# Hybrid decoder step: the output projection's LRU half on operands without the norm's root, and softplus of dt on 128 partitions by way of DRAM

## The reference, cut to what matters

```
xn = rmsnorm(h);  proj = xn @ w_in  ->  z, xbc, dt, gate, xl
xbc = silu(causal_conv(xbc));  dt = softplus(dt + dt_bias)       # 16 heads
a_cs = cumsum(dt * -exp(a_log)) per chunk of 128 tokens (per sample of 4)
y = SSD scan of xbc with dt and a_cs;  y_ssd = rmsnorm(y * silu(z))
xl = causal_conv(xl);  r, i = sigmoid(block gates of xl)
hs = linear recurrence, a = exp(-8 * r * softplus(-lambda))
y_lru = rmsnorm(hs * gelu(gate), norm_lru)                       # width 1024
h = h + concat(y_ssd, y_lru) @ w_out
h = h + PEER experts(rmsnorm(h));  h = h + gated embedding;  final rmsnorm
```

## Time and profile before

| what | value |
|---|---|
| median of 3 runs | 1906.53 us |
| the profiled execution | 1902.72 us |
| its span in the trace | 1901.0 us |
| PE busy | 1796.1 us (94%) |
| DVE busy | 1507.3 us (79%) |
| ACT busy | 837.1 us (44%) |
| the mixer's last matmuls | about 446 to 449 us |

### The profile page before, as it was taken

One profiled execution on the slowest core, in us unless ns is written; L12 is line 12 of the kernel. 1 busy time (PEld: TensorE's weight loads), 2 busy tenths in 40 slices (PEclk: granted clock), 3 DMA queues, 4 the chain that ended last, 5 costly groups with the idle time before them and its releaser, 6 DMA issues.

```text
span 1901.0 us, 29713 instructions
## 1 busy us (share of the span) xinstructions
PE 1796.1 (94%) x11394; PEld 1732.9 (91%) x11394; DVE 1507.3 (79%) x2723; ACT 837.1 (44%) x1202; POOL 522.0 (27%) x415
## 2 busy tenths in 40 slices
...
GB/s 143 91 67 79 116 118 99 51 56 179 112 128 146 145 169 227 234 295 345 361 362 373 352 353 359 367 392 376 380 367 380 376 394 379 375 338 340 205 56 48
DMA packets 163772, 462.68 MB, mean 243 GB/s; under 512 B 16624, under 2 KB 76720, under 8 KB 160944
## 3 DMA queue, kind: packets, MB, share of 16 engines
...
...
## 4 chain that ended last, share of the span: by engine, by line
PE 71%; DVE 13%; DMA 10%; ACT 3%; issue 2%; SPq 0%; POOL 0%; DVEq 0%; ACTq 0%
PE PS L454 12%; PE PS L1477 8%; PE PS L1478 7%; PE PS L1479 7%; DMA Rw<-vn 7%; PE PS L1490 6%; PE PS L1492 6%; PE PS L1491 6%; PE PS L1466 5%; PE PS L1543 4%; PE PS L2049 2%; DVE Hl L1853 1%; ACT Rh L164 1%; DVE Rl L169 1%; DVE ug L1861 1%
## 5 line engine op out<-in xcount | busy, mean ns | idle before, releaser
L169 DVE TENSOR_TENSOR Rl<-Rw,Rh 128x1024 fp32r<-128x1024 f32 x272 | 332.4, 1223 | 162.2 <-ACT Rh L164 154.8
L164 ACT CAST Rh<-Rw 128x1024 fp32r<-128x1024 f32 x272 | 284.1, 1045 | 389.4 <-PE PS L1492 343.8
L1432 POOL DMA_INDIRECT ug<-un,idxU x160 | 241.6, 1510 | 579.7 <-DVE dots L1861 353.9
L1490 PE MATMUL PS<-Hh,Rh 128*128 128x384 f32 x1024 | 352.2, 344 | 39.3 <-DVE Hl L1853 39.0
L1477 PE MATMUL PS<-Xh,Rh 128*128 128x384 f32 x1016 | 351.2, 346 | 3.8 <-DVE Rl L169 2.8
L1491 PE MATMUL PS<-Hl,Rh 128*128 128x384 f32 x1024 | 349.2, 341 | 0.0
L1492 PE MATMUL PS<-Hh,Rl 128*128 128x384 f32 x1024 | 349.0, 341 | 0.0
L1478 PE MATMUL PS<-Xl,Rh 128*128 128x384 f32 x1016 | 342.3, 337 | 0.0
L1479 PE MATMUL PS<-Xh,Rl 128*128 128x384 f32 x1016 | 341.3, 336 | 0.0
L1432 POOL DMA_INDIRECT ug<-vn,idxU x160 | 234.1, 1463 | 280.6 <-DVE yacc L1866 215.8
L1490 PEld LDWEIGHTS PS<-Hh,Rh 128*128 128x128 f32 x1024 | 194.9, 190 | 48.7 <-issue 48.5
...
## 6 DMA issues: line engine op xcount, KB each, us to landing
...
Rw<-vn SPq DMA_DIRECT2D x128, 512.0 KB
...
acts<-Ab SPq DMA_DIRECT2D x128, 192.0 KB
...
```

The lines of the kernel that those rows point to most:

```text
L164: a.copy(self.Rh[:, q, :], self.Rw[:, q, :]).then_inc(self.S("rhi"), 1)
L169: v.tensor_tensor(self.Rl[:, q, :], self.Rw[:, q, :], self.Rh[:, q, :].bitcast(F32), ALU.subtract).then_inc(self.S("rlo"), 1)
L1432: p.indirect_dma_start(out=ug[:, r % 4, :], out_offset=None, in_=un if r < IDC else vn, in_offset=bass.IndirectOffsetOnAxis(ap=idxU[:, r % ...
L1490: pe.matmul(out, Rh[:, q, w], hh, start=(g == 0), stop=False)
```

## The change

Softplus: `dts` is written to DRAM and read back so that 16 rows of 544 become 128 rows of 68 (`dtw[:, 6]`), and the result goes back the same way into `dts`. SP issues the first pair of transfers behind its load of tile 3, the second behind its load of tile 8, and waits within each pair. ACT's and DVE's parts stand one or two passes later (3, 4, 5, 6); product, scan and `wts` stay on 16 partitions and stand in pass 8, the exponentials of `wts` in pass 9.

LRU half: `ylh` and `yll` are made from `gg` times `norm_lru` alone; `lru_add` becomes two DVE operations, the PSUM result times `rstdL` into `tmpL`, and the sum with h. The squares 0 to 3 are taken in pass 21 (`sq4l`), DVE adds six of the eight squares (`lru_sum`) and PE sums three inputs behind tile 27. `BTb` and `CBs` stand ahead of `scores(0)` in pass 35, `CBm` in pass 32.

```diff
@@ -212,7 +212,8 @@
-    dtw = at("dtw", A5, [NH, 6, T])
+    dtw = at("dtw", A5, [P, 7, T // 8])
+    dA = at("dA", A5 + T * 4, [NH, T])
     smask = at("smask", A5 + 6 * T * 4, [NH, T])
@@ -240,6 +241,8 @@
     sq8l = at("sq8l", AT + SL, [P, ND, T])
+    sq4l = at("sq4l", A5, [P, 4, T])
+    tmpL = at("tmpL", sh.free + 2 * SL + T * 4, [P, T])
     ce = at("ce", A6, [P, 2, HG, P])
@@ -287,6 +292,16 @@
             load(n)
+            if n == 3:
+                sp.wait_ge(S("dt_v"), 2)
+                sp.dma_start(dtd, dts[:, :]).then_inc(S("dtm"), 16)
+                sp.wait_ge(S("dtm"), 16)
+                sp.dma_start(dtw[:, 6, :], dtd.rearrange("h (q t) -> (h q) t", q=8)).then_inc(S("dtm"), 16)
+            if n == 8:
+                sp.wait_ge(S("spv"), 19)
+                sp.dma_start(spd.rearrange("h (q t) -> (h q) t", q=8), dtw[:, 5, :]).then_inc(S("dtm"), 16)
+                sp.wait_ge(S("dtm"), 48)
+                sp.dma_start(dts[:, :], spd).then_inc(S("dtm"), 16)
             if n == 4:
@@ -427,7 +442,7 @@
             elif n < OS0:
-                pe.wait_ge(S("ole"), n - OL0 + 1)
+                pe.wait_ge(S("ole"), 2 * (n - OL0) + 1)
             else:
@@ -478,6 +493,15 @@
+        def lru_sums():
+            pe.wait_ge(S("sqz"), ND + 4)
+            pe.wait_ge(S("sq_ready"), 2 * ND)
+            for src, first, last in ((tmpL[:, :], True, False), (sq8l[:, 6, :], False, False),
+                                     (sq8l[:, 7, :], False, True)):
+                for q in range(2):
+                    m = pe.matmul(pair(3)[:, q, :], ones[:, :], src[:, q * HT:(q + 1) * HT], start=first, stop=last)
+            m.then_inc(S("sq_free"), ND)
+
         def sums(r, k, src):
@@ -601,9 +625,8 @@
                 token_scalars()
-            if n == 26:
-                for k in range(ND):
-                    sums(1, k, sq8l[:, k, :])
+            if n == 27:
+                lru_sums()
             if n == 28:
@@ -668,6 +691,8 @@
                 a.wait_ge(S("loo"), 4)
+            if i == ND + 2:
+                a.wait_ge(S("sqz"), ND + 2)
             a.activation(dst[:, 0:NP], ctmp[:, s, 0:NP], func).then_inc(S("act_c"), 1)
@@ -697,6 +722,9 @@
             a.activation(dst, src, ACT.Square).then_inc(S("sq_ready"), 1)
+
+        def lru_hi(k):
+            a.activation(ylh[:, k, :], gg[:, k, :], ACT.Copy, scale=col("norm_lru", k)).then_inc(S("ylh"), 1)
@@ -737,27 +765,25 @@
                 hi(n + 1)
-            if n == 2:
+            if n == 3:
                 a.preload_act_table(ACT.Exp)
-                a.wait_ge(S("dt_v"), 2)
-                a.activation(dtw[:, 0, :], dts[:, :], ACT.Abs).then_inc(S("spa"), 1)
+                a.wait_ge(S("dtm"), 32)
+                a.activation(dtw[:, 0, :], dtw[:, 6, :], ACT.Abs).then_inc(S("spa"), 1)
                 a.activation(lv[:, 0, :], col("lam", 0, ND), ACT.Abs).then_inc(S("spa"), 1)
...
                 a.activation(hv[:, 2:3], hv[:, 1:2], ACT.Exp).then_inc(S("spa"), 1)
-            if n == 4:
+            if n == 5:
                 a.wait_ge(S("spv"), 2)
...
                 a.activation(lv[:, 2, :], lv[:, 1, :], ACT.Ln).then_inc(S("spa"), 1)
-            if n == 7:
+            if n == 9:
                 a.wait_ge(S("spv"), 26)
...
             if GA0 < n <= ZZ0:
-                if n == GA0 + 1:
-                    a.wait_ge(S("spv"), 27)
                 sigmoids(n - GA0 - 1)
@@ -794,11 +820,18 @@
                     root(m)
+                a.wait_ge(S("ylr"), 4)
+                for k in range(4):
+                    lru_hi(k)
+                    square(1, k, sq4l[:, k, :], gg[:, k, :])
             if n == 25:
                 a.wait_ge(S("scan"), ND)
-                for k in range(ND):
+                for k in range(4, ND):
                     a.wait_ge(S("ylr"), k + 1)
                     square(1, k, sq8l[:, k, :], gg[:, k, :])
+            if n == 27:
+                for k in range(4, ND):
+                    lru_hi(k)
             if n in (26, 27):
@@ -809,10 +842,6 @@
                 a.preload_act_table(ACT.Silu)
-            if n in (31, 32):
-                for k in range(4 * (n - 31), 4 * (n - 31) + 4):
-                    a.wait_ge(S("normed"), k + 1)
-                    a.copy(ylh[:, k, :], gg[:, k, :]).then_inc(S("ylh"), 1)
             if n == 30:
@@ -944,15 +973,18 @@
-        def lru_norm(k):
-            v.wait_ge(S("rst"), 2)
-            v.scalar_tensor_tensor(out=gg[:, k, :], in0=gg[:, k, :], scalar=col("norm_lru", k), in1=rstdL[:, :],
-                                   op0=ALU.mult, op1=ALU.mult).then_inc(S("normed"), 1)
-
         def lru_lo(k):
             v.wait_ge(S("ylh"), k + 1)
-            v.tensor_tensor(yll[:, k, :], gg[:, k, :], ylh[:, k, :].bitcast(F32), ALU.subtract
-                            ).then_inc(S("yll"), 1)
+            v.wait_ge(S("sq_ready"), ND + k + 1)
+            v.scalar_tensor_tensor(out=yll[:, k, :], in0=gg[:, k, :], scalar=col("norm_lru", k),
+                                   in1=ylh[:, k, :].bitcast(F32), op0=ALU.mult, op1=ALU.subtract
+                                   ).then_inc(S("yll"), 1)
+
+        def lru_sum(k):
+            v.wait_ge(S("sq_ready"), ND + k + 1)
+            v.wait_ge(S("sqz"), ND + k - 2)
+            v.tensor_tensor(tmpL[:, :], sq4l[:, 0, :] if k == 1 else tmpL[:, :],
+                            sq4l[:, k, :] if k < 4 else sq8l[:, k, :], ALU.add).then_inc(S("sqz"), 1)
@@ -1015,8 +1047,12 @@
             v.wait_ge(S("mm"), n + 1)
-            hs = halves(h[:, d, :])
-            v.tensor_tensor(hs, hs, pair(n % 2), ALU.add).then_inc(S("ole"), 1)
+            v.wait_ge(S("rst"), 2)
+            if d >= 1:
+                v.wait_ge(S("ole"), 2 * d)
+            v.tensor_tensor(halves(tmpL[:, :]), pair(n % 2), halves(rstdL[:, :]), ALU.mult).then_inc(S("ole"), 1)
+            v.wait_ge(S("ole"), 2 * d + 1)
+            v.tensor_tensor(h[:, d, :], h[:, d, :], tmpL[:, :], ALU.add).then_inc(S("ole"), 1)
@@ -1135,15 +1170,18 @@
                 v.wait_ge(w, 18)
-                v.scalar_tensor_tensor(out=dts[:, :], in0=dts[:, :], scalar=0.0, in1=dtw[:, 5, :], op0=ALU.max,
-                                       op1=ALU.add).then_inc(w, 1)
+                v.scalar_tensor_tensor(out=dtw[:, 5, :], in0=dtw[:, 6, :], scalar=0.0, in1=dtw[:, 5, :],
+                                       op0=ALU.max, op1=ALU.add).then_inc(w, 1)
                 v.tensor_tensor(lv[:, 5, :], lv[:, 5, :], lv[:, 6, :], ALU.add).then_inc(w, 1)
                 v.wait_ge(w, 20)
-                v.tensor_scalar(dtw[:, 4, :], dts[:, :], hv[:, 3:4], None, ALU.mult).then_inc(w, 1)
                 v.tensor_scalar(spl[:, 0, :], lv[:, 5, :], -8.0, None, ALU.mult).then_inc(w, 1)
                 v.tensor_scalar(spl[:, 1, :], lv[:, 5, :], 8.0, None, ALU.mult).then_inc(w, 1)
+            if n == 8:
+                v.wait_ge(S("dtm"), 64)
+                v.tensor_scalar(dA[:, :], dts[:, :], hv[:, 3:4], None, ALU.mult).then_inc(w, 1)
                 v.wait_ge(w, 23)
-                v.tensor_tensor_scan(out=acs[:, :], data0=smask[:, :], data1=dtw[:, 4, :], initial=0.0, op0=ALU.mult,
+                v.wait_ge(S("const"), 28)
+                v.tensor_tensor_scan(out=acs[:, :], data0=smask[:, :], data1=dA[:, :], initial=0.0, op0=ALU.mult,
                                      op1=ALU.add).then_inc(w, 1)
@@ -1195,19 +1233,31 @@
                                   xs[r, 9, NP:T].rearrange("p (b t) -> p b t", b=NB)).then_inc(S("bcz"), 1)
-            if n in (30, 31):
-                for k in range(4 * (n - 30), 4 * (n - 30) + 4):
-                    lru_norm(k)
-            if n in (32, 33):
-                for k in range(4 * (n - 32), 4 * (n - 32) + 4):
-                    lru_lo(k)
+            if n in (24, 25):
+                lru_lo(2 * n - 48)
+                lru_lo(2 * n - 47)
+            if n == 25:
+                for k in range(1, 4):
+                    lru_sum(k)
+            if n == 26:
+                lru_sum(4)
+                lru_sum(5)
+            if n in (28, 30):
+                lru_lo(n - 24)
+                lru_lo(n - 23)
             if n == 33:
                 l_min(0)
+            if n == 32:
                 for b in range(2):
...
                                     mask[:, :].unsqueeze(1).broadcast_to([P, 4, P]), ALU.mult).then_inc(S("cbm"), 1)
+            if n == 35:
+                v.wait_ge(S("cbp"), 4)
+                v.tensor_tensor(CBs[:, :], PS[0:64, 6, 0:32], mask2[:, :], ALU.mult).then_inc(S("cbm"), 1)
+                v.tensor_tensor(BTb[:, :, :], PS[0:64, 6, P:2 * P].unsqueeze(1).broadcast_to([64, NB, P]),
+                                segm[:, :].unsqueeze(2).broadcast_to([64, NB, P]), ALU.mult).then_inc(S("cbm"), 1)
             if n == 35:
```

More of the change, by code:

```diff
@@ L1219, in vector @@
                 v.tensor_tensor(Ls[:, :, :], Ls[:, :, :], am, ALU.subtract).then_inc(S("lss"), 1)
-            if n == 35:
-                v.wait_ge(S("cbp"), 4)
```

(3 more changed lines are left out.)

25 lines of the change are left out of this document (13 added, 12 removed).

## The result

The changed kernel takes 1886.42 us (median of 4 runs, 1884.01 to 1890.32) beside 1906.1 us for the kernel before (4 runs, 1904.52 to 1908.59): ratio 0.9900, 95% interval 0.9877 to 0.9923. The forecast was 1890.5, with a range of 1884.5 to 1898.5. The profiled execution took 1887.0 us, its span is 1885.3: 15.7 us less than before's 1901.0, where 16.0 were forecast.

A forecast was written before the change was run, and what follows sets the result against it. PE, carrying 71% of the chain of waits, was taken as the bound, with the change in the mixer. 5.4 + 13.2 - 1.7 - 0.65 - 0.3 = 16.0 us off the median 1906.53 gave 1890.5, range 1884.5 to 1898.5.

The forecast's parts named there:

- Softplus: Tiles 3 to 10: softplus on 128 partitions removes PE's waits ahead of tiles 5 and 7; gain 5.4 us.
- The straight line between the two reciprocals: Softplus on DVE: interpolating 3.54 us for 544 columns and 0.13 for 8 gives 0.51 us for 68.
- Up to chunk 1's transposes: LRU half: fewer sums, less DVE work, earlier `BTb`; chunk 0 17.8 us ahead, chunk 1 13.2 ahead.
- Clock before tile 37: After chunk 1's transposes: PE, idle for 5 us, begins tile 37 at the lower clock; -1.7 us.
- Step (e): Behind 300 us: `lru_add`'s second DVE operation is hidden, except at the `ce` wait (-0.65 us) and ahead of tile 43 (-0.3).
- Tile 43: Ahead of tile 43, where PE waits for `yl`: the chain over `Wlo` is 0.3 us later.
- Behind the mixer: From about 460 us on: this part is shifted as a whole, with no gain of its own.
- B: Rival: tile 4's weight load lands late, PE waits 6.8 us and the clock drops; 1898 us, chance 0.12.
- C: Rival: DVE stays late in tiles 25 to 36, PE waits some 4 us, clock drops once; 1896 us, chance 0.08.
- D: Rival: no clock drop before tile 37 and shorter waits; gain 18 to 21 us, 1886 to 1888.5, chance 0.12.
- E: Rival: the later stages, paced by the experts' DMA, take the gain back, leaving below 4 us; chance 0.05.
- F: Rival: the clock stays down after the 4.4 us wait ahead of the `xs` transposes; slower, 1915 us, chance 0.03.

The follow-up runs named there:

- E5: Kernel before with the softplus steps in the change's new passes, but on 16 partitions and without the trip to DRAM: 1900.27 us, ratio 0.9977.
- E2: Kernel before with the LRU half and the moves of `BTb`, `CBs` and `CBm`, softplus as it was: 1894.61 us, ratio 0.9948.
- E3: Kernel before with only `CBs` and `BTb` moved ahead of `scores(0)` in DVE's pass 35: 1903.07 us, ratio 0.9998.
- E10: Changed kernel with PE summing all eight squares and DVE's additions left out: 1889.08 us, ratio 0.9919.
- E9: Changed kernel with two extra writes of `dts` to DRAM, waited for ahead of tile 4's load: 1889.94 us, ratio 0.9932.
- E4: Changed kernel with `BTb` and `CBs` put back behind `scores(0)`, `l_min(1)` and `Ls`: 1881.74 us, ratio 0.9895.
- E1: Kernel before with only the softplus part of the change (buffers, four transfers, passes): 1893.45 us, ratio 0.9935.
- E0: Changed kernel run again, unedited, on the same chip as its three variants: 1884.22 us, ratio 0.9917.
- E8: Changed kernel with chunk 3's `ce` transfer one tile earlier and chunk 0's state copy ahead of `scores(1)`, run twice: 1877.96 and 1878.12 us.
- E6: Changed kernel with SP issuing chunk 3's `ce` transfer behind the load of tile 40, not 41: 1883.90 us, ratio 0.9912.
- E7: Changed kernel with chunk 0's state copy ahead of `scores(1)` and `l_min(2)` in DVE's pass 36: 1884.43 us, ratio 0.9916.

## Why the prediction was right, and where it was not

- **Softplus, forecast 5.4.** Measured at the first gate 6.5, of which 0.5 was there already when tile 3 started (32.44, 31.96): 6.0. E5 shows that the new place alone doesn't make it. The mis-sized term is the trip to DRAM: I took the one `acsd` of the earlier trace rows, 2.8 us, and the four trips took 1.5 to 1.7. That price belonged to the moment and not to the transfer. In the kernel before, E2 and E3 SP issues `acsd` directly behind the load of a weight tile (0.5 us later), and it takes 2.8 to 3.1 us; in the other eleven traces it is issued about 3 us behind that load and takes 1.6. The Trainium skill (DMA: Bandwidth & Descriptors, Anatomy of one DMA), with about 2.0 us for the fixed part, was nearer than that row; by the measurement the figure is a little high for 34 KB, and the page gives it for transfers that GpSimd issues, where these are SP's. Of the 1.0 us of waiting that the price implied at most 0.2 came, and 0.4 in E10; E9 brought a wait back by adding the missing time. The straight line between the two reciprocals (0.51) held: 0.58.
- **Up to chunk 1's transposes, forecast 13.2.** Measured 19.3 less 6.5: 12.8. Chunk 0 was forecast at 257 with a wait of 4.4 (256.72, 4.36), chunk 1 16.6 later (16.54). What that step says of causes is shown by E10 (4.6 us of sums, whole) and by E3 and E4 (the order of `BTb`: 1.6 or 1.7 at chunk 1, nothing later). The 3.79 us ahead of tile 35 are gone in all kernels with the LRU half, and stand in E1, E3 and E5.
- **Clock before tile 37, forecast -1.7.** Chunk 2's gain is 2.2 below chunk 1's (2.8 in E0). The drop is confirmed by its absence in E4 and E8, where the wait ahead of chunk 1 is 0.74 and 0.76 (the tile behind it at 1.00).
- **Step (e), the chain over `ce`, forecast -0.65: this step failed.** It assumed that the transfer lands as fast as before. DVE's row had 6.32 us of waiting, and the chain ended 0.1 us ahead of PE: I added the one DVE operation of 0.7 and nothing for the transfer. Both halves of the chain were longer. SP issued the transfer 9.8 us behind the start of chunk 2's transposes, 8.6 before: 0.8 is the second DVE operation, and 0.4 lies between SP's load of the weight tile and its issue of the transfer (303.93 to 304.71), where before had

```profile
320.21 0.33 SPq L270 DMA_DIRECT2D Wr<-wm  x1
320.58 1.09 SPq L273 DMA_DIRECT2D ce<-eacd  x2
```

These 0.4 us stand in E1 too, and not in E2 or E9; what makes them is not shown. And from the first issue to DVE's read it was 6.9 us in this trace (304.71 to 311.63), and 5.9 in that of before. In the chain of waits the second of the two transfers stands as

```profile
305.21 6.39 DMA ce<-eacd
```

where before's two took 4.9 and 5.4 us, and E0's second one 5.59; 2 MB for `s0s` are issued right behind it in both kernels, and why it landed later is not shown. The late issue is in both traces of the changed kernel; the landing was 1.0 us slower than before in the first and 0.2 in E0: the wait for PE was 2.28, 1.49, 2.39 and 2.59 us in the changed kernel's two traces, E9 and E10. In all four the lower clock followed (0.67 to 0.83 over 10 us), which (e) did not count. Together 2.2 us at the transposes and up to 2.9 more by tile 43. E6 takes the chain away, and both parts of the loss with it.
- **Tile 43, forecast -0.3.** The wait is 2.44 in place of 2.18, as forecast. The lower clock behind it was not: the wait of 2.44 or 2.45 stands in all ten traces with the LRU half, and the granted clock over the 8 us behind it was 0.79 in six of them (the changed kernel, E7, E8 twice, E9, E10) and 1.00 in E0, E2, E4 and E6. It cost 1.5 us in the changed kernel (tile 43's gain of 12.0 is 10.4 at the last matmul), and nothing in E0. The mixer's sum as measured is 6.5 + 12.8 - 2.2 - 2.2 - 2.9 - 1.5, which makes 10.4 with unrounded terms, where 16.0 was forecast.
- **Behind the mixer, forecast 0.** This stretch was 5.3 us shorter. Over the 14 traces of this study it lies between 1445.2 (E4) and 1458.0 (E2), though its code is the same. PE's longest group of waits there, for `Hl` of the experts, moves along with it on the whole. That row is, for the kernel before, the changed kernel, E4 and E2:

```profile
PE PS L1490 <- DVE Hl L1853: 39.0, 13, 17.5
```
```profile
PE PS L1535 <- DVE Hl L1898: 35.8, 15, 15.3
```
```profile
PE PS L1535 <- DVE Hl L1898: 32.6, 13, 15.1
```
```profile
PE PS L1522 <- DVE Hl L1885: 41.2, 17, 16.0
```

(us in total, times, longest). The kernels whose mixer ends early have the shorter stretch on the whole (E8 1446.0 and 1448.7, E3 1457.4, E5 1455.1), but E9 has 1457.6, E1, with a late mixer, 1450.5, and E4, with a later mixer than E8, 1445.2. E0 came to 1449.8, within 0.5 of the first trace: that is what the rival of its expectation asked for (a property of this kernel), though E9, with the same code there, is 8 us off. The times of all runs bear on it too. Taken as us (the ratio's interval times the median before), the first set gave 14.7 to 23.4 us less, E1 7.8 to 17.1, both above what the mixer gave in the traces (10.4 to 13.4, and 3.9); E0's 11.2 to 20.3 takes in its 13.4. So more than the mixer's gain is there in the mean of the runs, and chance alone is the less likely reading; what in the experts would gain from an earlier start, no run here shows, and it stays open. It also sets how far the forecast of 1890.5 was right for its reasons: by the mixer alone, with its 10.4 to 13.4 us, the changed kernel would be at 1893 to 1896 from a median of 1906.5.

Of the rivals, B (late load) did not come, though E9 shows how near it was; C did not; D failed at its condition, since the clock did drop, though the median lies in D's band (1886 to 1888.5); E, that the later stages take the gain back, did not come: the stretch behind was shorter, not longer. F, the clock staying down, was given 0.03 as it had no row. E7 has one: nearly 21 us at the lower level with PE never idle, some 10 us of work lost. The Trainium skill (TensorE: Matmul & The Clock Gate, Part 1) reports a clock seen stuck low for over 50 us, as a caveat on trace data; here it was less than half of that, in one trace of 14, and the 84 matmuls in place of 140 show that the work was slower. E7's time in all came out equal to E0's. F's reading that the drops of the trace before each lasted 3.4 us also leaves out the third: behind the wait of 11.47 us the granted clock was 0.75 over 10 us (280.49 to 290.49), 5 us at the lower level.
